# Delta rule on one core: two groups of heads half a level apart, products of one beside those of the other

## The chip, the cores and the metric

One core of a Trainium2 chip runs the whole program. The time is device microseconds of one execution; the median of three runs of the kernel before is 2759.25 us (2759.2 to 2761.63).

## The reference, cut to what matters

Two decoder layers run over 1024 tokens. The second one mixes tokens with the gated delta rule: eight heads, keys and values 128 wide. Each chunk solves a unit lower triangular system and passes a state on to the next chunk.

```python
a_mat = eye + where(strict, einsum('bhnid,bhnjd->bhnij', kb, k) * decay, 0)
sol = triangular_solve(a_mat, rhs, lower=True, unit_diagonal=True)   # -> u, w
attn = where(tri, einsum('bhnid,bhnjd->bhnij', q, k) * decay, 0)
def step(state, inp):
    v_new = u_n - w_n @ state
    o_n = qd_n @ state + attn_n @ v_new
    state = state * exp(gl_n) + kd_n^T @ v_new
```

The output o is divided by its root mean square, weighted, gated and projected.

## The kernel before, in words

`delta_rule` (from L4524) works in eight chunks of 128 tokens. All eight heads are on the chip together, in two groups of four (`q` = 0, the low group, heads 0 to 3; `q` = 1, the high group, heads 4 to 7). The inverse X of a chunk's triangular matrix is built by doubling: it begins with 2x2 blocks on the diagonal and joins pairs of blocks in six levels (`LEVELS`). For the first five levels a matrix of 128 rows is held as two blocks of 64, one on partitions 0 to 63 (`low`), one on 64 to 127 (`high`). A product of 64x64 operands uses one quarter of TensorE's array: its rows are the partitions that the operands lie on, its columns the partitions that the result is written to. A quarter is straight if both are the same half, and crosses if they differ. A quarter that crosses moves a block to the other half.

One level has two kinds of product. `products_b` (L4701, matmuls at L4716, at the last level L4713) multiplies B, the rest of the matrix, by X; `x_blk` holds X's blocks in the other half than `xt_blk` holds the transpose's, so all B products cross. `products_x` (L4719) multiplies the masked result by X's transpose, once straight (D, L4734) and once crossing (E, L4736), so it uses all four quarters; at the last level it is one crossing product per head (L4731). Each 64x64 product in float32 is two records in the trace, each with a weight load of its own.

Between them VectorE works, group by group: `mask_products` (L4981) takes B's result out of PSUM, times a mask, into `t_m`; `join` (L4989) subtracts E from `x_blk` (L4997) and D from `xt_blk` (L4998). At the last level `mask_products` is L4984 and `join` copies to `xt` (L4995).

The order on TensorE is written out by hand (from L4793). Per level both groups' B come first, then a block of other work, then both groups' X, then another such block. The blocks are 128-wide products for the same chunk, the next one or the one before: `k_state` (L4747) at levels 1 and 2, `outputs` of chunk n - 1 (L4760, L4761) at levels 2 and 3, `kk` of chunk n + 1 (L4671) at levels 3 and 4, `qk` (L4676) at levels 4 and 5. At the last level `first_x` (L4689, matmuls L4698) copies the next chunk's start into `first_ps` by products with the identity; `turn_out` (L4775, L4782) transposes the gated output of chunk n - 1; `new_values` (L4764, L4772) makes the chunk's new values; then come B of the next chunk's level 1 and `key_values` (L4785, L4790).

VectorE's order (from L5025) follows that of TensorE: both masks, other work, both joins. The other work is `next_state` (L5012) at level 1, `rests` (L5005) around levels 1 and 2, `sum_outputs` (L5014, a reduction of 128x1024 at L5018) behind level 3's joins, `decayed_keys` of chunk n + 1 (L4973) at level 4, `decayed_queries` (L4979) at levels 5 and 6.

ScalarE copies the outputs (`copy_y`, L4862), squares them (L4868), later scales the gated output (`finish_outputs`, L4892), moves B across the halves (`move_blocks`) and copies `first_ps` to `x_blk` (`copy_x`, L4917). GpSimd gates the output (`gate_outputs`, L5106), scales the next queries (L5076), computes the norm from the sum of squares (`output_norm`, L5112 and L5114), and only then makes the next chunk's first blocks (`start`, L5091 and L5093), which `first_x` waits for. All orders are fixed; engines wait for one another by semaphores alone, and an engine's queue stands still behind a wait.

Of the kernel before, what the change touches and what calls it, by code (L numbers as in the profile page):

```python
# [9 lines left out]
P = 128  # L10
# [4494 lines left out]
LEVELS = 6  # L4505
BLK = P // 2
# [17 lines left out]
def delta_rule(nc, feat, kv, gc_rows, gate_dram, norm_w, upper, ident, gates, gate_stored, kv_stored, a, following, chunk, late):  # L4524
# [14 lines left out]
    with ExitStack() as ctx:  # L4539
# [32 lines left out]

        t_ps, d_ps, e_ps, first_ps, last_ps = ([halves[:, b + q, e] for q in range(2)]
                                               for b, e in ((0, 0), (2, 0), (0, 1), (2, 1), (0, 1)))
        v_ps, c_ps, d4_ps = fours[2:4], fours[4:6], fours[6:8]
# [42 lines left out]
        def in_group(q):  # L4618
            return range(q * HG, (q + 1) * HG)

        @block.sync
# [43 lines left out]
        def _(pe):  # L4665
# [19 lines left out]
            def qk(m, q):  # L4685
                qk_opens(m, q)
                qk_heads(m, q, slice(0, HG)).then_inc(qk_done, 1)

            def first_x(m):  # L4689
                pe.wait_ge(start_done, m + 1)  # L4690
                if m > 0:
                    pe.wait_ge(x_joined, JV * m)
                    pe.wait_ge(xt_done, LV * m - 2)
                pe.sem_inc(tiles_seen, 1)
                for q in range(2):
                    for h in in_group(q):
                        for half, across in halves_across:
                            mm = pe.matmul(first_ps[q][across, h % HG], xt_blk[half, m % 2, h], ident[half, half], start=True, stop=True)  # L4698
                    mm.then_inc(x_done, 1)

            def products_b(n, l, q):  # L4701
                if l == 1:
                    pe.wait_ge(x_copied, 2 * n + q + 1)
                    pe.wait_ge(b_moved, 4 * n + 2 * q + 2)
# [5 lines left out]
                b = b_across[:, n % 2]  # L4710
                for h in in_group(q):
                    if l == LEVELS:
                        mm = pe.matmul(t_ps[q][high, h % HG], b[high, h, high], x_blk[high, h], start=True, stop=True)  # L4713
                    else:
                        for half, across in halves_across:
                            mm = pe.matmul(t_ps[q][half, h % HG], b[across, h, half], x_blk[across, h], start=True, stop=True)  # L4716
                mm.then_inc(t_done, 1)

            def products_x(n, l, q):  # L4719
                s = n % 2  # L4720
                pe.wait_ge(tm_done, LV * n + 2 * (l - 1) + q + 1)
                if l == 1:
                    pe.wait_ge(x_copied, 2 * n + 2)
                    if n > 0:
                        pe.wait_ge(v_copied, 2 * (n - 1) + q + 1)
                else:
                    pe.wait_ge(xt_done, LV * n + 2 * (l - 2) + q + 1)
                pe.sem_inc(tiles_seen, 1)
                for h in in_group(q):
                    if l == LEVELS:  # L4730
                        mm = pe.matmul(last_ps[q][low, h % HG], t_m[high, h], xt_blk[high, s, h], start=True, stop=True)  # L4731
                    else:
                        for half in (low, high):
                            pe.matmul(d_ps[q][half, h % HG], t_m[half, h], xt_blk[half, s, h], start=True, stop=True)  # L4734
                        for half, across in halves_across:
                            mm = pe.matmul(e_ps[q][across, h % HG], xt_blk[half, s, h], t_m[half, h], start=True, stop=True)  # L4736
                mm.then_inc(d_done, 1)

            def k_state(n, q):
# [34 lines left out]

            def turn_out(n):  # L4775
                pe.wait_ge(y_done, H * (n + 1))
# [4 lines left out]
                for h in range(H):  # L4781
                    mm = pe.transpose(c_both[:, h], gated[:, h], ident[:])  # L4782
                mm.then_inc(y_turned, 1)

# [13 lines left out]
            first_x(0)  # L4798
            for q in range(2):
                products_b(0, 1, q)  # L4800
            for n in range(TT):
                more = n + 1 < TT
                if n > 0:
                    for q in range(2):
                        key_values(n - 1, q)
                for l in range(1, LEVELS + 1):
                    if l > 1:
                        for q in range(2):
                            products_b(n, l, q)
                    if l == 2:  # L4810
                        k_state(n, 1)
                    if l == 3 and n > 0:
                        outputs(n - 1, 1)
                    if l == 4 and more:
                        kk(n + 1, 1)
                    if l == 5 and more:
                        qk_opens(n + 1, 1)
                        qk_heads(n + 1, 1, slice(0, HG // 2))
                    if l == LEVELS and more:
                        first_x(n + 1)  # L4820
                    for q in range(2):
                        products_x(n, l, q)
                    if l == 5 and more:
                        qk_heads(n + 1, 1, slice(HG // 2, HG)).then_inc(qk_done, 1)
                    if l == 1:
                        k_state(n, 0)
                    if l == 2 and n > 0:
                        outputs(n - 1, 0)
                    if l == 3 and more:
                        kk(n + 1, 0)  # L4830
                    if l == 4 and more:
                        qk(n + 1, 0)
                    if l == LEVELS and n > 0:
                        turn_out(n - 1)
                for q in range(2):
                    new_values(n, q)
                if more:
                    for q in range(2):
                        products_b(n + 1, 1, q)
            for q in range(2):  # L4840
# [3 lines left out]
        def _(act):  # L4844
# [72 lines left out]
            def copy_x(m):  # L4917
                if m > 0:
                    act.wait_ge(t_done, LV * m)
                for q in range(2):  # L4920
                    act.wait_ge(x_done, 2 * m + q + 1)
                    act.copy(group(x_blk, q), first_ps[q]).then_inc(x_copied, 1)

# [35 lines left out]
        def _(dve):  # L4959
# [21 lines left out]
            def mask_products(n, l, q):  # L4981
                dve.wait_ge(t_done, LV * n + 2 * (l - 1) + q + 1)
                if l == LEVELS:
                    dve.tensor_scalar(group(t_m[high], q), t_ps[q][high], -1.0, None, ALU.mult).then_inc(tm_done, 1)  # L4984
# [4 lines left out]
            def join(n, l, q):  # L4989
                s = n % 2  # L4990
                dve.wait_ge(d_done, LV * n + 2 * (l - 1) + q + 1)
                if l == LEVELS:
                    if n > 0:
                        dve.wait_ge(v_done, 2 * n)
                    dve.tensor_copy(group(xt[low, :, high], q), last_ps[q][low]).then_inc(xt_done, 1)  # L4995
                else:
                    dve.tensor_tensor(group(x_blk, q), group(x_blk, q), e_ps[q], ALU.subtract).then_inc(x_joined, 1)  # L4997
                    dve.tensor_tensor(group(xt_blk[:, s], q), group(xt_blk[:, s], q), d_ps[q], ALU.subtract).then_inc(xt_done, 1)  # L4998

# [25 lines left out]
            for n in range(TT):  # L5025
                more = n + 1 < TT
                for l in range(1, LEVELS + 1):
                    for q in range(2):
                        mask_products(n, l, q)
                    if l == 1 and n > 0:  # L5030
                        for q in range(2):
                            next_state(n - 1, q)
                    if l == 2:
# [3 lines left out]
                    if l == 5 and more:  # L5037
                        decayed_queries(n + 1, 0)
                    for q in range(2):
                        join(n, l, q)  # L5040
                    if l == LEVELS and more:
                        decayed_queries(n + 1, 1)
                    if l == 1:
                        rests(n, 0)
                    if l == 3 and n > 0:
                        sum_outputs(n - 1)
                    if l == 4 and more:
                        decayed_keys(n + 1, 1)
            following.split_lo(dve)

# [347 lines left out]
```

## Time and profile before

| | |
|---|---|
| median of three runs | 2759.25 us |
| the profiled execution, its own time | 2758.13 us |
| its span, first to last instruction | 2756.3 us |
| TensorE (PE) busy | 2673.5 us, 97% |
| VectorE (DVE) busy | 2116.3 us, 77% |
| ScalarE (ACT) busy | 1283.5 us, 47% |
| GpSimd (POOL) busy | 327.4 us, 12% |

The delta rule lies between about 1744 and 2002 us. In such rows stand the start in us from the span's first instruction, the duration, the engine, the line of the code, the operation with output and inputs, the shape and the number of instructions merged. PE is a matmul, PEld its weight load. A matmul's row ends when its result is written, so that successive rows overlap: the distance between starts tells what a product costs. What stands in square brackets at the end of a row is the engine's idle time before it and who ended it; "issue" means that the profile shows nothing that was waited for.

### The profile page before, as it was taken

Reading aid. Unit: us, or ns where it says so; the run is one execution under the profiler, and the core shown is the slowest. Engines: PE = TensorE matmul, PEld = TensorE weight load, DVE = VectorE, ACT = ScalarE, POOL = GpSimd, SP = SyncE. Lnnn points to the kernel's source line nnn. Section 1 sums busy time; section 2 is a strip of 40 time slices with the busy share of each in tenths; the row PEclk is TensorE's granted clock in tenths of the full one; section 3 lists DMA queues with packets and bytes.
Section 4 is the critical chain, followed back from the end, with each engine's and each line's share of the span. In section 5 each row is a group of like instructions: output and inputs, shape, how many; then the busy total and the mean of one; then the engine's idle time right before and its main releaser. Section 6 shows DMA issues by size and latency. Waiting matters only on the chain. (4 is left out here: it accounts for less than half of the span.)

```text
span 2756.3 us, 45813 instructions
## 1 busy us (share of the span) xinstructions
PE 2673.5 (97%) x17883; PEld 2240.5 (81%) x17883; DVE 2116.3 (77%) x3278; ACT 1283.5 (47%) x2296; POOL 327.4 (12%) x257
## 2 busy tenths in 40 slices
PE   9999989989999999999999999999999999999998
PEld 7888877778888888888878887888878888888886
DVE  6644456875799999897999975466658999998978
ACT  5333336842454444443456744566543544444332
POOL 0000045240000000000000001466411000000001
PEclk9999999999999999999999999999999999999999
DMA  5333253633412222475223423522042122225652
GB/s 186 122 107 107 92 195 114 170 123 110 147 54 92 85 81 80 159 265 187 92 93 121 158 76 123 196 95 96 16 176 101 69 92 77 84 92 188 226 185 88
DMA packets 162448, 339.15 MB, mean 123 GB/s; under 512 B 35584, under 2 KB 69568, under 8 KB 151616
## 3 DMA queue, kind: packets, MB, share of 16 engines
q1 hardware_dynamic: 144528, 324.69, 33.5%
q10 hardware_dynamic: 17712, 11.60, 1.4%
q8 instruction: 141, 2.31, 0.3%
q14 instruction: 67, 0.55, 0.1%
HBM read 252.17 MB, written 84.05 MB: 122 GB/s over the span
## 5 line engine op out<-in xcount | busy, mean ns | idle before, releaser
L2496 POOL TENSOR_TENSOR ffn_down_rstd<-ffn_down_rstd,ffn_down_power 128x1 f32<-128x1 f32 x15 | 15.0, 1000 | 1263.5 <-DVE ffn_down_rstd L2432 1263.5
L1053 DVE TENSOR_TENSOR even_in_w_lo<-even_in_raw_left,even_in_w_hi 128x512 fp32r<-128x512 f32 x80 | 49.9, 686 | 88.2 <-ACT even_in_w_hi L978 88.2
L936 PE MATMUL even_in_acc<-even_in_w_hi,even_x_hi 128*128 128x512 f32 x256 | 99.6, 389 | 0.0
L937 PE MATMUL even_in_acc<-even_in_w_lo,even_x_hi 128*128 128x512 f32 x256 | 99.6, 389 | 0.0
L938 PE MATMUL even_in_acc<-even_in_w_hi,even_x_lo 128*128 128x512 f32 x256 | 99.6, 389 | 0.0
L4040 DVE SCALAR_TENSOR_TENSOR even_mixed<-even_mixed,odd_qkv_taps 128x1023 f32<-128x1023 f32 (+2 forms) x72 | 92.1, 1281 | 4.9 <-ACT even_mixed L3873 3.2
L938 PE MATMUL even_in_acc<-even_in_w_hi,even_in_s_lo 128*128 128x512 f32 x192 | 74.7, 389 | 0.0
L936 PE MATMUL even_in_acc<-even_in_w_hi,even_in_s_hi 128*128 128x512 f32 x192 | 74.7, 389 | 0.0
L937 PE MATMUL even_in_acc<-even_in_w_lo,even_in_s_hi 128*128 128x512 f32 x192 | 74.7, 389 | 0.0
L3524 DVE CUSTOM_DVE_ANT_0 dil_probs<-dil_bank,dil_mask 128x128 f32<-128x128 f32 (+1 forms) x192 | 56.1, 347 | 22.3 <-PE dil_bank L3432 16.4
L3480 ACT ACTIVATE dil_probs<-dil_probs,dil_neg_peak 128x128 f32<-128x128 f32 (+1 forms) x192 | 70.7, 442 | 1.8 <-DVE dil_neg_peak L3529 1.8
L994 ACT COPY even_in_stage<-even_in_acc 128x512 f32<-128x512 f32 x48 | 28.2, 587 | 90.4 <-PE even_in_acc L938 83.2
L978 ACT CAST even_in_w_hi<-even_in_raw_left 128x512 fp32r<-128x512 f32 x80 | 43.7, 620 | 56.9 <-PE even_in_acc L938 56.9
L1225 ACT ACTIVATE odd_mixed<-odd_mixed,ffn_up_taps 128x1024 f32<-128x1024 f32 x44 | 54.5, 1245 | 32.9 <-DVE odd_mixed L1526 20.9
L1225 ACT ACTIVATE even_mixed<-even_mixed,ffn_up_taps 128x1024 f32<-128x1024 f32 x44 | 54.5, 1245 | 31.7 <-DVE even_mixed L1526 20.9
L4986 DVE TENSOR_TENSOR gdn_t_m<-gdn_bank,gdn_first_joins 128x256 f32<-128x256 f32 x80 | 33.2, 422 | 40.4 <-PE gdn_bank L4716 38.3
L2323 PE MATMUL ffn_down_acc<-four_hi,ffn_open_hi 128*128 128x512 f32 x160 | 62.3, 389 | 1.5 <-PEq L64 1.5
L2323 PE MATMUL ffn_down_acc<-two_hi,ffn_open_hi 128*128 128x512 f32 x160 | 62.4, 390 | 1.2 <-PEq L64 1.2
L1332 PE MATMUL ffn_up_tiles_acc<-ffn_up_tiles_t_hi,three_hi 128*128 128x512 f32 x160 | 62.4, 390 | 0.6 <-DVE three_lo L1490 0.6
L1332 PE MATMUL ffn_up_tiles_acc<-ffn_up_tiles_t_hi,one_hi 128*128 128x512 f32 x160 | 62.4, 390 | 0.6 <-DVE one_lo L1490 0.6
L2325 PE MATMUL ffn_down_acc<-two_hi,ffn_open_lo 128*128 128x512 f32 x160 | 62.3, 389 | 0.0
L2325 PE MATMUL ffn_down_acc<-four_hi,ffn_open_lo 128*128 128x512 f32 x160 | 62.3, 389 | 0.0
(877 smaller groups left out, 9095.6 us busy)
## 6 DMA issues: line engine op xcount, KB each, us to landing
ffn_w_raw<-in_ffn_up SPq DMA_DIRECT2D x42, 1024.0 KB, 4.8
even_mixed<-in_ffn_down SPq DMA_DIRECT2D x28, 512.0 KB, 4.4
odd_mixed<-in_ffn_down SPq DMA_DIRECT2D x28, 512.0 KB, 3.8
hp<-even_in_stage SPq DMA_DIRECT2D x13, 1024.0 KB, 4.2
hidden<-even_mixed SPq DMA_DIRECT2D x22, 512.0 KB, 2.6
ffn_w_raw<-in_od_w_qkv SPq DMA_DIRECT2D x11, 1024.0 KB, 5.7
hidden<-odd_mixed SPq DMA_DIRECT2D x22, 512.0 KB, 2.6
even_in_raw_left<-in_ev_w_in SPq DMA_DIRECT2D x10, 1024.0 KB, 5.3
```

What stands on the lines that cost most here:

```text
L936: pe.matmul(to, hi[:, tok], wh, start=(opens and k == 0), stop=False, skip_group_check=not opens)
L937: pe.matmul(to, hi[:, tok], wl, start=False, stop=False, skip_group_check=not opens)
L938: mm = pe.matmul(to, lo[:, tok], wh, start=False, stop=(k == KH - 1), skip_group_check=not opens)
L978: act.copy(w_hi[:, p % 2, k], source(i)[:, k]).then_inc(hi_ready, 1)
L1053: dve.tensor_tensor(w_lo[:, p % 2, k], source(i)[:, k], f32(w_hi[:, p % 2, k]), ALU.subtract).then_inc(lo_ready, 1)
L1225: act.activation(conv[:, g], c[:, g], ACT.Identity, bias=tap(j, g, FFN_CONV), scale=tap(j, g, FFN_CONV - 1)).then_inc(tap_done, 1)
L1332: mm = pe.matmul(result(m, i), ww[:, k], xx[:, k], start=(k == 0 and n == 0), stop=(k == KH - 1 and n == 2))
L2323: pe.matmul(bank(i, t), ah[:, tok], wh, start=begins, stop=False, skip_group_check=not opens)
L2325: return pe.matmul(bank(i, t), al[:, tok], wh, start=False, stop=ends, skip_group_check=not opens)
L3480: act.activation(p, p, ACT.Exp, bias=neg_peak[:, u % 2, h]).then_inc(exp_done, 1)
L3524: dve.tensor_tensor_reduce(probs[:, u % 2, h, k], s_ps[h][:, k], mask[:, kind(u), k], 1.0, -3e38, ALU.add, ALU.max, peak[:, u % 2, h]).the ...
L4040: dve.scalar_tensor_tensor(out=conv[:, g, back:SEQ], in0=c[:, g, 0:SEQ - back], scalar=tap(tile, GDN_CONV - 1 - back), in1=conv[:, g, back ...
```

## The change

Heads 0 and 1 become straight heads: their `x_blk` stays in its own half, so that their B products run on straight quarters and their E products too, with results in PSUM places of their own (`t_first`, `t_straight`, `t_last`, `e_straight`). `copy_x` takes heads 0 and 1 in one copy and the other six in another. On VectorE the low group's masks and x joins become two instructions each.

On TensorE the two groups are half a level apart. `low_x_high_b(n, l)` issues the low group's X and the high group's B of level l, alternating; `high_x_low_b(n, l)` issues the high group's X of level l and then the low group's B of level l + 1. Between these two stand the blocks of other work, in the order as before. At the last level the low group's B and X come earlier than the high group's; `turn_out` is cut in two, one half behind each of the two B or X groups; `key_values` of the high heads waits for the first mask, since `t_first` lies in its bank. VectorE's order becomes group by group as well, and `sum_outputs` stands behind level 4's low join.

```diff
+        first_ps = [bank[:, 2 + i].rearrange("p (h t) -> p h t", t=BLK) for i in range(2)]
+        e_straight, t_straight, t_first, t_last = halves[:, 2, 1], halves[:, 3, 1], halves[:, 7, 0], halves[:, 1, 0]
...
+            def b_head(n, l, h):
+                for half, across in halves_across:
+                    if straight(h):
+                        mm = pe.matmul(t_to(l, h)[half], b_mat[half, n % 2, h, half], x_blk[half, h], start=True, stop=True)
+                    else:
+                        mm = pe.matmul(t_to(l, h)[half], b_across[across, n % 2, h, half], x_blk[across, h], start=True, stop=True)
+                return mm
...
+            def e_head(n, h):
+                for half, across in halves_across:
+                    to = e_straight[half, h] if straight(h) else e_ps[h // HG][across, h % HG]
+                    mm = pe.matmul(to, xt_blk[half, n % 2, h], t_m[half, h], start=True, stop=True)
+                return mm
...
+            def high_x_low_b(n, l):
+                high_x(n, l)
+                if l == 1 and n > 0:
+                    pe.wait_ge(v_copied, 2 * n)
+                products_b_open(n, l + 1, 0)
+                b_head(n, l + 1, 0)
+                b_head(n, l + 1, 2)
+                b_head(n, l + 1, 1)
+                b_head(n, l + 1, 3).then_inc(t_done, 1)
+
+            def low_x_high_b(n, l):
+                products_x_open(n, l, 0)
+                pe.sem_inc(tiles_seen, 1)
+                d_head(n, 0)
+                e_head(n, 2)
+                d_head(n, 1)
+                e_head(n, 3)
+                products_b_open(n, l, 1)
+                d_head(n, 2)
+                b_head(n, l, 4)
+                d_head(n, 3)
+                b_head(n, l, 5)
+                e_head(n, 0)
+                b_head(n, l, 6)
+                e_head(n, 1).then_inc(d_done, 1)
+                b_head(n, l, 7).then_inc(t_done, 1)
...
                 if n > 0:
-                    for q in range(2):
-                        key_values(n - 1, q)
...
+                    key_values(n - 1, 0)
+                    pe.wait_ge(tm_done, LV * n + 1)
+                    key_values(n - 1, 1)
+                low_x(n, 1)
+                k_state(n, 0)
+                high_x_low_b(n, 1)
+                k_state(n, 1)
+                low_x_high_b(n, 2)
+                if n > 0:
+                    outputs(n - 1, 0)
+                high_x_low_b(n, 2)
...
+                low_x_high_b(n, 5)
+                if more:
+                    qk_heads(n + 1, 1, slice(HG // 2, HG)).then_inc(qk_done, 1)
+                high_x(n, 5)
+                last_b(n, 0)
+                if n > 0:
+                    turn_out(n - 1, 0)
+                last_x(n, 0)
+                last_b(n, 1)
+                if more:
+                    first_x(n + 1)
+                last_x(n, 1)
+                if n > 0:
+                    turn_out(n - 1, 1)
...
+                join_x(n, 1, 0)
+                join_xt(n, 1, 0)
+                rests(n, 0)
+                for l in range(2, LEVELS):
+                    mask_products(n, l, 0)
+                    join_x(n, l - 1, 1)
+                    join_xt(n, l - 1, 1)
                     if l == 2:
                         rests(n, 1)
                     if l == 4 and more:
                         decayed_keys(n + 1, 0)
                     if l == 5 and more:
                         decayed_queries(n + 1, 0)
...
+                    dve.wait_ge(d_done, LV * n + 2 * (l - 1) + 1)
+                    mask_products(n, l, 1)
+                    join_x(n, l, 0)
+                    join_xt(n, l, 0)
+                    if l == 4 and n > 0:
                         sum_outputs(n - 1)
                     if l == 4 and more:
                         decayed_keys(n + 1, 1)
+                mask_products(n, LEVELS, 0)
+                join_x(n, LEVELS - 1, 1)
+                join_xt(n, LEVELS - 1, 1)
+                if more:
+                    decayed_queries(n + 1, 1)
+                join_last(n, 0)
+                mask_products(n, LEVELS, 1)
+                join_last(n, 1)
```

`low_x` is `low_x_high_b` without B (level 1), `high_x` the high group's X as before, `last_b` and `last_x` the last level's products of one group, `first_b` level 1's B of both.

## Rows read from the trace of the kernel before

**Rows 1.** The page's first line.

```profile
span 2756.3 us, 45813 instructions
```

**Rows 2.** Timeline of TensorE in a middle chunk, levels 3 and 4.

```profile
1862.12 0.39 PE L4761 MATMUL gdn_bank<-gdn_v_new,gdn_attn 128*128 128x128 f32 x2
1862.43 0.27 PE L4734 MATMUL gdn_bank<-gdn_xt_blk,gdn_t_m 64*64 64x64 f32 x2
...
1862.49 0.14 PEld L4734 LDWEIGHTS gdn_bank<-gdn_xt_blk,gdn_t_m 64*64 64x64 f32 x2
...
1863.37 0.23 PE L4736 MATMUL gdn_bank<-gdn_t_m,gdn_xt_blk 64*64 64x64 f32 x2
1863.53 1.16 PE L4671 MATMUL gdn_bank<-gdn_first_x_t 128*128 128x128 f32 x8
1864.62 1.15 PE L4716 MATMUL gdn_bank<-gdn_x_blk,gdn_b_across 64*64 64x64 f32 x32
1865.69 1.16 PE L4671 MATMUL gdn_bank<-gdn_first_x_t 128*128 128x128 f32 x8
```

**Rows 3.** The same timeline: the same chunk's first_x, and a quiet chunk's ends.

```profile
1874.12 0.27 PE L4698 MATMUL gdn_bank<-top_ident,gdn_xt_blk 64*64 64x64 f32 x2
...
1938.94 1.95 PE L4772 MATMUL gdn_bank<-gdn_u,gdn_xt 128*128 128x128 f32 x16
...
1966.08 1.15 PE L4698 MATMUL gdn_bank<-top_ident,gdn_xt_blk 64*64 64x64 f32 x32 [0.37 <-POOL gdn_xt_blk L5093]
...
1969.02 1.95 PE L4772 MATMUL gdn_bank<-gdn_u,gdn_xt 128*128 128x128 f32 x16
```

**Rows 4.** Timelines of ACT, POOL and DVE beside rows 2, the same chunk.

```profile
1862.54 0.58 ACT L4862 COPY gdn_y<-gdn_bank 128x512 f32<-128x512 f32 x1 [2.47 <-PE gdn_bank L4761]
...
1863.26 2.37 POOL L5106 TENSOR_TENSOR gdn_gated<-gdn_y,gdn_gate 128x1024 f32<-128x1024 f32 x1 [2.02 <-issue]
1865.59 2.37 POOL L5076 TENSOR_TENSOR gdn_q_et<-gdn_first_x_t,gdn_exp_row 128x1024 f32<-128x1024 f32 x1
1867.91 0.20 POOL L5112 TENSOR_TENSOR gdn_o_norm<-gdn_o_sumsq,top_q_eps 128x8 f32<-128x8 f32 x1
1868.19 1.65 POOL L5114 TENSOR_TENSOR gdn_o_norm<-gdn_o_norm,gdn_power 128x8 f32<-128x8 f32 x1
1870.01 2.62 POOL L5091 TENSOR_TENSOR gdn_xt_blk<-gdn_b_mat,gdn_first_c 64x512 f32<-64x512 f32 x2 [0.17 <-POOL gdn_o_norm L5114]
1872.71 1.27 POOL L5093 TENSOR_TENSOR gdn_xt_blk<-gdn_xt_blk,gdn_unit_c 128x512 f32<-128x512 f32 x1
...
1863.20 0.42 DVE L4997 TENSOR_TENSOR gdn_x_blk<-gdn_x_blk,gdn_bank 128x256 f32<-128x256 f32 x1 [2.20 <-PE gdn_bank L4736]
1863.54 0.41 DVE L4998 TENSOR_TENSOR gdn_xt_blk<-gdn_xt_blk,gdn_bank 128x256 f32<-128x256 f32 x1
...
1864.53 1.21 DVE L5018 TENSOR_REDUCE gdn_o_sumsq<-gdn_squares 128x8 f32<-128x1024 f32 x1
```

**Rows 5.** Timelines of TensorE and DVE: first and last chunk's v products, a mask and its X.

```profile
1783.91 2.02 PE L4772 MATMUL gdn_bank<-gdn_u,gdn_xt 128*128 128x128 f32 x16 [0.24 <-DVE gdn_xt L4995]
...
1996.87 1.95 PE L4772 MATMUL gdn_bank<-gdn_u,gdn_xt 128*128 128x128 f32 x16
...
1990.63 0.42 DVE L4986 TENSOR_TENSOR gdn_t_m<-gdn_bank,gdn_first_joins 128x256 f32<-128x256 f32 x1
...
1991.19 0.27 PE L4734 MATMUL gdn_bank<-gdn_xt_blk,gdn_t_m 64*64 64x64 f32 x2
```

**Rows 6.** Timeline of TensorE: an idle time that the profile ascribes to nothing.

```profile
1872.43 0.21 PE L4734 MATMUL gdn_bank<-gdn_xt_blk,gdn_t_m 64*64 64x64 f32 x1 [0.61 <-issue]
```

**Rows 7.** Groups of instructions kept apart by shape, VectorE, another stage's masking from PSUM.

```profile
L3524 DVE CUSTOM_DVE_ANT_0 dil_probs<-dil_bank,dil_mask 128x256 f32<-128x256 f32 x88 | 32.0, 419 | 10.8 <-PE dil_bank L3432 9.4 <-DVE dil_gathered L3569 1.3 <-PE dil_bank L3423 0.2
L3524 DVE CUSTOM_DVE_ANT_0 dil_probs<-dil_bank,dil_mask 128x128 f32<-128x128 f32 x104 | 24.0, 285 | 11.5 <-PE dil_bank L3432 7.1 <-DMA dil_mask<-in_dil_masks 3.4 <-DVE dil_part L3569 1.0
```

More of the change, by code:

```diff
@@ new lines, in d_head @@
+            def d_head(n, h):
+                for half in (low, high):
+                    pe.matmul(d_ps[h // HG][half, h % HG], t_m[half, h], xt_blk[half, n % 2, h], start=True, stop=True)
+            def e_head(n, h):
+                for half, across in halves_across:
+                    to = e_straight[half, h] if straight(h) else e_ps[h // HG][across, h % HG]
+                    mm = pe.matmul(to, xt_blk[half, n % 2, h], t_m[half, h], start=True, stop=True)
+                return mm
@@ L4728, in products_x, with last_x @@
+            def last_x(n, q):
+                products_x_open(n, LEVELS, q)
                 pe.sem_inc(tiles_seen, 1)
                 for h in in_group(q):
[L4730 to L4736, printed above, removed]
@@ L4737, in products_x @@
-                mm.then_inc(d_done, 1)
+                    mm = pe.matmul(last_ps[q][low, h % HG], t_m[high, h], xt_blk[high, n % 2, h], start=True, stop=True)
+                mm.then_inc(d_done, 1)
+            def high_x_low_b(n, l):
[7 more added lines that the diff above has]
+                b_head(n, l + 1, 3).then_inc(t_done, 1)
@@ L4798, in _ @@
             first_x(0)
-            for q in range(2):
-                products_b(0, 1, q)
+            first_b(0)
             for n in range(TT):
@@ L4919, in copy_x @@
                     act.wait_ge(t_done, LV * m)
-                for q in range(2):
-                    act.wait_ge(x_done, 2 * m + q + 1)
-                    act.copy(group(x_blk, q), first_ps[q]).then_inc(x_copied, 1)
+                for i, some in enumerate((slice(0, 2), slice(2, H))):
+                    act.wait_ge(x_done, 2 * m + i + 1)
+                    act.copy(x_blk[:, some], first_ps[i][:, some]).then_inc(x_copied, 1)
             def copy_out(n):
@@ L4983, in mask_products @@
                 if l == LEVELS:
-                    dve.tensor_scalar(group(t_m[high], q), t_ps[q][high], -1.0, None, ALU.mult).then_inc(tm_done, 1)
+                    if q == 0:
+                        dve.tensor_scalar(t_m[high, 0:2], t_last[high, 0:2], -1.0, None, ALU.mult)
+                    some = slice(2, HG) if q == 0 else slice(0, HG)
+                    dve.tensor_scalar(group(t_m[high], q)[:, some], t_ps[q][high, some], -1.0, None, ALU.mult).then_inc(tm_done, 1)
+                elif q == 0:
+                    mask = joins[:, l - 1].unsqueeze(1).broadcast_to([P, 2, BLK])
+                    dve.tensor_tensor(t_m[:, 0:2], (t_first if l == 1 else t_straight)[:, 0:2], mask, ALU.mult)
+                    dve.tensor_tensor(t_m[:, 2:HG], t_ps[0][:, 2:HG], mask, ALU.mult).then_inc(tm_done, 1)
                 else:
```

158 lines of the change are left out of this document (87 added, 71 removed).

## The prediction

> **What bounds the kernel now.** I read the page first: the profiled execution spans 2756.3 us [rows 1], the time beside it is 2758.13 us, and the sum below is made against that 2758.13; it lies 1.1 us under the median of the runs, 2759.25. The change touches one stage, the delta rule, eight chunks of 128 tokens. Second, TensorE's timeline in one chunk [rows 2]. The reader is to see that there is no idle time: X products run from 1862.43, the last pair starts at 1863.37, the 128-wide block of the next chunk's keys follows at 1863.53, B at 1864.62, the next block at 1865.69. The 64 X records (two per product) take 0.94 us, 0.0585 us for every four; the 32 B records take the same time, since B uses only the two quarters of the array that cross from one half of the partitions to the other. I call 0.0585 us a step: X of both groups is 16 steps, B of both groups 16. A level is X, a block of other work, B and another such block: 1.10, 1.09, 1.07 and again 1.09, so 4.35 us [rows 2].
>
> Third, the end of a chunk [rows 3]. In the quiet chunk between the first v product at 1938.94 and the next at 1969.02 (30.08 us) TensorE does wait once: first_x at 1966.08, 0.37 us, for POOL's xt_blk. So I read the other engines along what leads there [rows 4]: the last output product of the chunk starts at 1862.12 [rows 2], ACT copies y at 1862.54, POOL gates it at 1863.26, scales the next queries at 1865.59, takes the norm at 1867.91 and its power at 1868.19, builds the next chunk's start from 1870.01 and 1872.71, ends it at 1873.98, and first_x comes 0.14 later, at 1874.12. That is 12.00 us from the last output to first_x, and first_x to the next chunk's outputs is TensorE alone. The stage is bound by a loop through both engines.
>
> To price the change I went through the orders of TensorE, VectorE, ScalarE and GpSimd as the code has them, each instruction with its duration from these rows: VectorE starts 0.27 to 0.29 after the last product it needs starts (the low group's X ends with the eighth step, at 1862.91; the join starts at 1863.20), 128x256 instructions leave 0.33 apart, a product starts 0.14 after the VectorE instruction it needs has ended (1991.05 to 1991.19) [rows 4, 5]. For the kernel before this gives 29.99 us per full chunk: 29.10 of TensorE's own work and 0.89 of waiting for POOL. The quiet chunk shows 30.08. The last chunk, which has no next chunk to fill its gaps, comes to 26.25. From the first chunk's v product to the last one's that is 206.31 us; the trace has 212.96 [rows 5]. The 6.65 us left over are idle times that no row explains, like the 0.61 before 1872.43 that ends by "issue" [rows 6].
>
> **The change, part by part.** *B beside X.* In levels 2 to 5 the low group's B runs in four quarters (4 steps instead of 8), and the high group's B runs on the quarters that the low group's X leaves free: 12 steps for both where 8 and 8 stood. A level is 24 steps, not 32: 8 x 0.0585 x 4 levels = 1.87 us per chunk. Level 1 gains nothing: its B saves 4 steps, its low X, with nothing beside it, loses 4. Products, weight loads and DMAs stay as many; no moved step issues a DMA, and SP's loads, which wait for keys, queries and gate of the chunk before, are released within 2 us of their old place and used a chunk later: nothing for them.
>
> *The transposes of the output in two halves.* One more change from 64-wide to 128-wide work and back: 0.15 in (1863.38 to 1863.53 [rows 2]), 0.21 back, an estimated 0.06 for the slower first step of each of the two blocks (the sixteenth step of X starts 0.94 after the first, where 15 steps are 0.88 [rows 2]), less the two steps that stood there, 0.15: 0.32 us. The low group's last B, half overlapping, saves a step. TensorE's own work falls by 1.87 - 0.32 + 0.06 = 1.61, from 29.10 to 27.49.
>
> *VectorE's halves.* Eleven instructions per chunk become two, since heads 0 and 1 lie in another bank. No row in this stage has that shape from PSUM; another stage's masking from PSUM takes 285 ns at 128x128 and 419 at 128x256 [rows 7], and 419 is also what the joins take here [rows 4]. I take 0.285 and starts 0.20 apart, the nearest row; a gain is excluded, a half costing a whole (0.42) is the upper end, which adds 4.5 us over the stage.
>
> *VectorE's new order, the part that decides.* The sum of squares (1.21 us, at 1864.53 [rows 4]) moves from behind level 3's joins to behind level 4's low join, and the group-wise order puts that join behind the mask of level 4's high group. Count from the last output product. TensorE: low X of level 3 from 0.20, keys, half-level from 2.13, keys, low X with high B of level 4 from 4.06 to 4.75. VectorE: mask at 5.02, the two half joins 5.35 and 5.55, the other join 5.75, the sum from 6.08 to 7.29. POOL would be free for the norm at 5.79 (1867.91 less 1862.12); before, the sum was done at 3.62 (1865.74). Now the norm starts at 7.34, and 6.21 later (1867.91 to 1874.12) first_x: 13.55 instead of 12.00. TensorE is there at 12.84 and waits 0.72. Behind the sum VectorE also has the key decay (0.62) and then level 5's low mask, done at 8.33; TensorE is free at 7.48 and starts low X of level 5 at 8.47: 0.99 of waiting, with qk, X and B of levels 5 and 6 queued behind. Smaller waits (0.05, 0.09, 0.20) follow at level 5's high B, its high X and level 6's low X. ScalarE's scaling of the gated output is 1.5 later with the norm; the transposes still find it done, by 0.4 us.
>
> The other half of the loop, first_x to the last output, loses 28 of 112 steps (8 of X that now stand ahead of first_x, 4 of B in level 1, 8 in each of the two rounds of X and B that follow: 1.64) and four transposes that now stand ahead of first_x (4 x 0.093): 17.99 becomes 15.97. So a chunk takes 15.97 + 13.56 = 29.53 against 29.99: 0.46 won out of 1.61. The added wait on the low group's mask between the two key-value blocks costs nothing: the mask is over 0.6 us before it.
>
> *The last chunk.* From level 3 no block covers VectorE's round trip. Before, one group's products cover the other's masks; now each half-level ends, then 0.27 + 0.42 + 0.14 pass, 0.77 more than a step, twice a level. Going through it the same way gives 27.34 against 26.25: 1.09 lost.
>
> *Sum.* 6 x 0.46 - 1.09 = 1.7 us less. The unexplained 6.65 I leave as it is: as many instructions in about the same time. 2758.13 - 1.7 = 2756.4, on the scale of the median 2757.6 us. A measurement of this kernel can tell about 0.2% (5.5 us) from no change, so this is no change.
>
> **A rule against it.** In the X block, weight loads for both kinds of product on the same rows run while products on those rows are under way (loads at 1862.49 between products that start at 1862.43 and last 0.27) and four records still pass per step [rows 2]. The Trainium skill, "TensorE: Matmul & The Clock Gate", Part 3, says that a weight load overlaps products in flight only where the row group differs; by it the other group's B would queue behind D and E on the same rows. The trace speaks against it for X, where D and E share rows.
>
> **The rivals.** *Unpaired B, slower.* If the high group's B doesn't run beside the low group's X, that half-level is 20 steps, not 12, and the loop comes to 30.94 a chunk: 10.3 us more than before, 2769.5 us. It decides (5.5 us slower) once some six in ten of these steps are unpaired. For it: two groups' operands were never mixed in one block. Against it: D, E and both halves mix at full rate now [rows 2]. Chance 0.10; it is also the case that the change doesn't do what it says.
>
> *The sum is not in the way, faster.* If VectorE reaches the sum earlier, or POOL is held by something else than the rows show, the two waits of 0.99 and 0.72 go and a chunk takes some 28.4: 9.3 us less, 2750 us. For it: this count rests on waits that no row of before shows. Against it: for the quiet chunk of before it is right to 0.1 us. Chance 0.16.
>
> *The unexplained idle time moves.* The blocks are denser now. If it falls from 6.65 to near nothing, 2751 (0.09); if it doubles, 2764.3, and with halves on VectorE at the price of a whole 4.5 more, 2768.8 (0.07).
>
> **How the numbers follow.** The forecast, within 5.5 us of the median, has 0.58. Faster 0.16 + 0.09 = 0.25, slower 0.10 + 0.07 = 0.17. The range takes in the two faster cases and the doubled idle time with a third of the dearer halves, 2749 to 2766, and leaves out the unpaired B.
>
> **What would show it.** Right: low X and high B as one run of 48 records in about 0.7 us; sum of squares ending about 7.3 us after the last output; first_x waiting for POOL in nearly every chunk; X of level 5 waiting for its mask about 1 us; chunks 29.5 apart when quiet; the last chunk longer than before. Wrong: that run at 1.0 us or more (unpaired), or POOL's norm starting under 6 us after the last output and chunks near 28.

## The result and the profile after

The changed kernel took 2766.36 us (median of 20 runs, 2753.68 to 2774.93), the kernel before 2760.72 in its 20 runs beside them: a ratio of 1.0022 with a 95% interval of 1.0013 to 1.0030. It is slower by 5.6 us where 1.7 us less and "no change" was forecast; the median lies 0.4 us above the range.

The first lines of the page after; [rows 1] is what answers to the span.

```profile
span 2763.5 us, 45876 instructions
...
PE 2671.2 (97%) x17883; PEld 2234.1 (81%) x17883; DVE 2119.3 (77%) x3366; ACT 1284.0 (46%) x2296; POOL 328.9 (12%) x257
```

TensorE is busy 2.3 us less and the span is 7.2 us longer. The timelines of TensorE, VectorE, GpSimd and ScalarE in one quiet chunk after, 1848.29 to 1878.30, answer to [rows 2 to 4]:

```profile
1848.29 0.35 PE L4857 MATMUL gdn_bank<-gdn_u,gdn_xt 128*128 128x128 f32 x1
...
1862.32 0.39 PE L4846 MATMUL gdn_bank<-gdn_v_new,gdn_attn 128*128 128x128 f32 x2
1862.64 0.27 PE L4731 MATMUL gdn_bank<-gdn_xt_blk,gdn_t_m 64*64 64x64 f32 x2
...
1863.34 0.23 PE L4726 MATMUL gdn_bank<-gdn_x_blk,gdn_b_across 64*64 64x64 f32 x2
1863.50 1.16 PE L4676 MATMUL gdn_bank<-gdn_first_x_t 128*128 128x128 f32 x8
...
1871.04 0.27 PE L4731 MATMUL gdn_bank<-gdn_xt_blk,gdn_t_m 64*64 64x64 f32 x2 [0.99 <-DVE gdn_t_m L5084]
...
1876.20 0.95 PE L4703 MATMUL gdn_bank<-top_ident,gdn_xt_blk 64*64 64x64 f32 x32 [0.71 <-POOL gdn_xt_blk L5212]
...
1878.30 0.35 PE L4857 MATMUL gdn_bank<-gdn_u,gdn_xt 128*128 128x128 f32 x1
...
1865.58 0.29 DVE L5083 TENSOR_TENSOR gdn_t_m<-gdn_bank,gdn_first_joins 128x128 f32<-128x128 f32 x1 [0.70 <-PE gdn_bank L4726]
...
1868.69 1.21 DVE L5125 TENSOR_REDUCE gdn_o_sumsq<-gdn_squares 128x8 f32<-128x1024 f32 x1
...
1869.98 0.20 POOL L5231 TENSOR_TENSOR gdn_o_norm<-gdn_o_sumsq,top_q_eps 128x8 f32<-128x8 f32 x1 [1.81 <-DVE gdn_o_sumsq L5125]
...
1877.89 0.65 ACT L5015 COPY gdn_x_blk<-gdn_bank 128x128 f32<-128x128 f32 x2
```

The mechanism is the predicted one. Low X and high B, 48 records, run from 1862.64 to the last pair at 1863.34, and the next block starts at 1863.50. The last output product is the two records of the row at 1862.32; the forecast's times count from the second, at 1862.43. The sum ends 7.47 us after it (forecast 7.29), POOL's norm starts after 7.55 (7.34) with 1.81 us of waiting for it, level 5's X waits 0.99 (0.99) for its mask, first_x 0.71 (0.72) for POOL. A half on VectorE takes 0.28 to 0.29 us (0.285). But the chunk takes 30.0 us, not 29.53.

Put side by side, the distances between the first v products of successive chunks, read from the timelines, the last one being the last chunk:

| kernel | us | sum |
|---|---|---|
| before | 30.59 31.37 31.18 31.26 30.62 30.08 27.85 | 212.96 |
| after | 34.04 32.67 30.02 33.02 31.36 30.02 29.62 | 220.74 |

The 7.8 us between the sums are all of the 7.2 by which the span grew. They are not in the quiet chunks, 30.08 and 30.02, but in the disturbed ones. Two things disturb them. The first is in the view of waits, TensorE alone, 1784 to 1990 us (us in total, times, longest); of after:

```profile
PE gdn_bank L4731 <- DVE gdn_t_m L5084: 6.2, 6, 1.3
PE gdn_bank L4857 <- issue: 3.8, 2, 2.5
PE gdn_bank L4703 <- POOL gdn_xt_blk L5212: 3.6, 5, 0.7
PE gdn_bank L4876 <- issue: 2.4, 2, 1.7
...
PE gdn_bank L4726 <- issue: 0.5, 1, 0.5
```

and of before:

```profile
PE gdn_bank L4734 <- issue: 2.5, 3, 1.2
PE gdn_bank L4716 <- issue: 1.8, 2, 1.5
PE gdn_bank L4736 <- issue: 1.5, 2, 1.3
PE gdn_bank L4734 <- DVE gdn_t_m L4986: 1.4, 1, 1.4
PE gdn_bank L4698 <- POOL gdn_xt_blk L5093: 1.0, 2, 0.6
...
PE gdn_bank L4747 <- issue: 0.3, 1, 0.3
```

Idle time by "issue", the kind of [rows 6], is 6.1 us of 9.0 before and 6.7 of 17.2 after, so it stayed; VectorE's and POOL's waits came on top. The second is the granted clock. The rows by windows (length, busy time of each engine, PEclk, DMA share, GB/s), of after:

```profile
1904.00:1911.00 7.00, 6.96 (x105) 6.24 (x105) 3.85 (x12) 5.39 (x13) 5.72 (x5) 0.52 0.80 255
...
1996.00:2007.00 11.00, 10.39 (x96) 9.63 (x97) 3.00 (x9) 5.09 (x13) 2.05 (x1) 0.53 0.01 1
```

and of before:

```profile
1904.00:1911.00 7.00, 7.00 (x119) 6.69 (x120) 3.39 (x10) 4.24 (x10) 2.90 (x3) 1.00 0.78 245
...
1996.00:2007.00 11.00, 8.62 (x66) 8.30 (x66) 4.13 (x6) 7.07 (x11) 0.00 (x0) 0.91 0.08 23
```

After, TensorE is granted 1.2 GHz for nearly all of these two stretches, just behind idle times (1.0 and 0.5 us in the 2.5 us up to 1903.41; 0.7 to 1.3 us five times in the last chunk before 1996); before, it keeps 2.4 GHz through the first and up to 2005.0 in the second. A third such stretch, 1788.2 to 1791.6, follows a single idle time of 1.74 us by "issue". From level 5's X to the next v product a chunk needs 6.96 us at 1.2 GHz (1904.36 to 1911.32) and 5.60 at 2.4 (1872.70 to 1878.30).

What is behind "issue"? The longest one cuts a run of eight equal v products (sixteen records), in a place where no new wait stands. TensorE's timeline after:

```profile
1815.62 1.69 PE L4857 MATMUL gdn_bank<-gdn_u,gdn_xt 128*128 128x128 f32 x13
1819.80 0.49 PE L4857 MATMUL gdn_bank<-gdn_u,gdn_xt 128*128 128x128 f32 x3 [2.50 <-issue]
```

and the DMA view of after, first from 1811 to 1817 us, then from 1817 to 1818.5 (queue and kind: packets, MB, share of 16 engines; a packet counts whole where it starts, so a share can pass 100%):

```profile
q1 hardware_dynamic: 2176, 1.97, 102.2%
...
q1 hardware_dynamic: 30, 0.13, 21.2%
q8 instruction: 1, 0.02, 4.5%
```

While x_t and x of a coming chunk, 2.1 MB, fill the sixteen engines, no packet of the instruction queue passes; the 16 KB of instructions come with the tail of the burst, ending at 1818.52, and the product follows 1.3 us later. It is the same everywhere: all fourteen idle times by "issue" between the first and the last v product, nine before and five after, end 1.3 to 1.6 us behind such a 16 KB packet, and each lies, counted in the trace, a multiple of 256 TensorE instructions (to within one) from the others of its kernel. That made the theory for the experiments: the late sum costs the waits, the chunk loads make TensorE's code late, and waits and late code together lower the clock. The trace of after already speaks against so simple a rule for the clock: from 1807 to 1820 idle times of 1.27, 0.75 and 2.50 us follow one another and it stays at 2.4 GHz. Rival: the idle time by "issue" is TensorE's own, and the sum alone decides.

### The profile page after: what moved, and what is told of

Read it like the earlier page. It is cut to its first block and busy times, and to the rows that moved or that the text cites. A ratio compares the mean times of both kernels' runs of the same rounds, so it can differ in the third digit from the quotient of the medians.

```text
span 2763.5 us, 45876 instructions
## 1 busy us (share of the span) xinstructions
PE 2671.2 (97%) x17883; PEld 2234.1 (81%) x17883; DVE 2119.3 (77%) x3366; ACT 1284.0 (46%) x2296; POOL 328.9 (12%) x257
## 5 line engine op out<-in xcount | busy, mean ns | idle before, releaser
L994 ACT COPY even_in_stage<-even_in_acc 128x512 f32<-128x512 f32 x48 | 28.3, 589 | 90.3 <-PE even_in_acc L938 83.7
L4731 PE MATMUL gdn_bank<-gdn_xt_blk,gdn_t_m 64*64 64x64 f32 x1280 | 56.3, 228 | 13.1 <-DVE gdn_t_m L5084 9.2
L4731 PEld LDWEIGHTS gdn_bank<-gdn_xt_blk,gdn_t_m 64*64 64x64 f32 x1280 | 45.6, 137 | 23.6 <-issue 17.0
L4736 PE MATMUL gdn_bank<-gdn_t_m,gdn_xt_blk 64*64 64x64 f32 x1280 | 62.7, 228 | 0.0
```

What stands on the lines that cost most here:

```text
L4731: pe.matmul(d_ps[h // HG][half, h % HG], t_m[half, h], xt_blk[half, n % 2, h], start=True, stop=True)
L4736: mm = pe.matmul(to, xt_blk[half, n % 2, h], t_m[half, h], start=True, stop=True)
```

## The experiments

Each run's kernel before ran on the same chip beside it.

**The sum of squares a level earlier**, in the changed kernel.

```diff
-                    if l == 4 and n > 0:
+                    if l == 3 and n > 0:
                         sum_outputs(n - 1)
```

> The changed kernel with the sum of squares back behind level 3 (behind the low group's join of level 3). Theory 1 (the late sum holds GpSimd and the masks, and the idle time on TensorE that follows costs its clock): the 1.26 us gap before level 5's low X and the 0.92 us gap before first_x close to under 0.4 us, quiet chunks are 28.1 us apart instead of 30.0, fewer stretches at half clock; 10 to 14 us faster than the changed kernel, some 6 to 10 faster than the kernel before (ratio to before 0.996 to 0.998). Theory 2 (denser TensorE work makes late starts without a cause, 'issue', more frequent): the gaps close, but the idle time ended by 'issue' grows by as much, and the time stays within 4 us of the changed kernel's.

Measured: 2760.37 us, ratio to before 1.0000 (0.9987 to 1.0013). Quiet chunks fell to 28.33 to 28.40 as expected, but four of seven took 31.1 to 31.6: the waits view has 7.7 us of "issue" here, and the last chunk ran at 1.2 GHz for 17 us. Moving the sum back is worth 6 us where 10 to 14 were expected; the idle time by "issue" is still there.

**The unfilled places filled**: two products with the identity matrix in the seven places of the first and the last chunk where no block of other work stands, their results overwritten.

```diff
+            def fill(n):
+                if n > 0:
+                    pe.wait_ge(y_copied, 2 * (n - 1) + 1)
+                for i in range(2):
+                    pe.matmul(d4_ps[0][:, i], ident[:], ident[:], start=True, stop=True)
...
+                else:
+                    fill(n)
```

> The changed kernel with two 128-wide products of the identity (unused result) in each of the seven places of the first and last chunk where no block of other work stands. Theory 1: these take the place of idle time that the walk already has (0.77 us each), so nothing is added; the clock stays at 2.4 GHz in the last chunk, whose distance falls from 29.6 to about 27.5 us, and the last outputs run in 3.4 us instead of 4.3; 3 to 5 us faster than the changed kernel, about even with the kernel before. Theory 2: no change, or slower by the products' own 4 us.

Measured: 2763.56 us, 1.0010 (0.9998 to 1.0021). The last chunk took 27.83 us, 1.8 less, and the stage ran 10 us at 1.2 GHz instead of 27. The clock is part of it; the middle chunks still took up to 33.6.

**Both together.**

> Both edits together. Theory 1: the gains add, 13 to 17 us faster than the changed kernel and 9 to 12 us faster than the kernel before (ratio 0.9955 to 0.997). Theory 2: within 4 us of the changed kernel.

Measured: 2760.39 us, 1.0001 (0.9990 to 1.0011). The two gains did not add up: quiet chunks 28.34, but others of 30.3 to 34.3. My expectation had left out that the code could be later still: its waits view has 10.9 us of "issue".

**The kernel before with the late sum** (behind level 4's joins).

```diff
-                if l == 3 and n > 0:
+                if l == 4 and n > 0:
                     sum_outputs(n - 1)
```

> The kernel before with one edit alone: the sum of squares behind level 4's joins instead of level 3's. Theory 1: chunks 32.05 us apart instead of 29.99 when quiet, with a wait of first_x for GpSimd of about 3 us in each; 13 us slower, and more if the clock falls in these waits, ratio 1.004 to 1.008. Theory 2: VectorE has idle time in this kernel, so the place of the sum costs nothing, ratio 1.000.

Measured: 2782.94 us, 1.0082 (1.0065 to 1.0099), so 22.6 us slower. In a middle chunk first_x now waits 2.01 us for POOL (about 3 was expected), and 37.5 us of the stage ran at 1.2 GHz. The place of the sum is a heavy price by itself, more than the waits alone.

**Small chunk loads**, in three kernels: the test of late code. From the third chunk on only 16 of 128 rows of x_t, x and the gate are fetched (the gate's lines are not shown); the rest is left out, so the stage computes with older data. gc_row, 0.5 MB, is loaded whole as ever.

```diff
-                sp.dma_start(x_t[:, s], feat[:, :, m * P:(m + 1) * P].rearrange("h d t -> d h t")).then_inc(x_t_in[s], 16)
+                rows = slice(0, P if m < 2 else 16)
+                sp.dma_start(x_t[rows, s], feat[:, rows, m * P:(m + 1) * P].rearrange("h d t -> d h t")).then_inc(x_t_in[s], 16)
...
-                sp.dma_start(x[:, s].rearrange("p h d -> p (h d)"), kv[m]).then_inc(x_in[s], 16)
+                sp.dma_start(x[rows, s].rearrange("p h d -> p (h d)"), kv[m][rows]).then_inc(x_in[s], 16)
```

> The kernel before, in which the loads of x_t, x and the gate for the chunks from the third on fetch 16 of 128 partitions (the other partitions keep the data of two chunks earlier, so the numbers computed are other ones; the instructions are the same). Theory 'late code': TensorE's idle time without a releaser, some 8 us between the first and the last new_values in the trace of before, is its next 16 KB of instructions held up behind 2.1 MB and 1 MB of chunk loads on the DMA engines. Without the load bursts the gaps of 0.8 to 1.8 us at the instruction blocks vanish, the chunks take 29.5 us each but the last, 206.3 in place of 212.96 us in all, and the time is 2753 to 2755 us. Rival 'the idle time is TensorE's own (its queue or its array)': the gaps stay, 2760 us.

> The changed kernel with the same small loads (the same part of the computation on older data). Theory 'late code and the clock': the late sum's waits (1.0 us before X5 low, 0.9 before first_x) stay in every chunk, the code gaps go; chunks of 30.0 us in place of 30.0 to 34.0, and the half clock follows only the unfilled places of the first and the last chunk: 2756 to 2760 us, still slower than the kernel before with small loads by some 2 to 5 us. If the waits alone set the half clock in the middle chunks, it stays and the time is 2763 us or more. Rival 'TensorE's own': 2766.

> The changed kernel with the sum of squares a level earlier, the seven unfilled places filled and the small loads (the same part of the computation on older data). Theory 'late code': all chunks but the first at 28.3 to 28.4 us and the last at 27.5, the sum from the first to the last new_values 197 to 199 us against 212.96, so 2744 to 2748 us: what the stagger saves is there as soon as the code comes in time. Rival 'what is won in a chunk is given back somewhere else': 2756 to 2760.

Measured: before 2752.54 us, 0.9975 (0.9964 to 0.9986); after 2756.04, 0.9985 (0.9976 to 0.9994); early and filled 2746.05, 0.9946 (0.9933 to 0.9959). The times are the theory's (the first 0.5 us under its range); the chunks in the trace of before with small loads are not, 30.06 us and more where 29.5 was expected. The waits view of after with small loads, the same stretch, whole:

```profile
PE gdn_bank L4734 <- DVE gdn_t_m L5087: 8.3, 8, 1.3
PE gdn_bank L4706 <- POOL gdn_xt_blk L5215: 4.3, 6, 0.7
PE gdn_bank L4734 <- DVE gdn_t_m L5089: 2.2, 3, 0.7
PE gdn_bank L4797 <- DVE gdn_t_m L5083: 0.8, 1, 0.8
PE gdn_bank L4870 <- ACT gdn_gated L4988: 0.2, 1, 0.2
```

No row by "issue" is left, and the waits of the late sum all are. Its chunks: 30.43, then 30.01 or 30.02 five times, and 28.14; those of before with small loads 30.06 to 30.17 but for one of 32.06, and 27.57 (some 3 us of "issue" remain there; the longest, 1.8 us, stands behind the burst of gc_row). With the early sum and the filled places they take 28.33 to 29.76, 1.5 us of "issue" among them, and 27.82. The rows by windows of after with small loads:

```profile
1777.00:1960.00 183.00, 170.43 (x4008) 153.92 (x4008) 116.62 (x325) 126.75 (x332) 117.91 (x73) 1.00 0.08 23
```

Six chunks with idle times of 1.0 and 0.7 us each, and the clock stays at 2.4 GHz. In this execution the waits alone don't lower it, nor in that of the changed kernel with paced loads below, from 1770 to 1981 us. But this one is the shortest of the eleven, 2749.03 us at a mean clock of 0.995; their median is 2756.04 at 0.993, an estimated 11 us more at 1.2 GHz (0.002 of 2756 us, at half the clock), and where in the program those lie no trace shows.

**The whole loads in pieces**: x_t and x in four parts, gate and gc_row in two, 256 KB each, and SP waits for the next B products of TensorE before each part (shown for x_t).

```diff
+            def after_products(n, l, q):
+                if LV * n + 2 * (l - 1) + q + 1 > 0:
+                    sp.wait_ge(t_done, LV * n + 2 * (l - 1) + q + 1)
...
+                for i in range(4):
+                    after_products(m - 3 + i // 2, 6 if i < 2 else 1, i % 2)
+                    cut = slice(i * H // 2, (i + 1) * H // 2)
+                    sp.dma_start(x_t[:, s, cut], feat[cut, :, m * P:(m + 1) * P].rearrange("h d t -> d h t")
+                                 ).then_inc(x_t_in[s], 16)
```

With the early sum and the filled places:

> The changed kernel with the sum of squares a level earlier, the seven places filled, and the whole chunk loads in twelve pieces of 256 KB (x_t in four, x in four, gate and gc_row in two each), each piece waiting for the next half level's B products of TensorE, so that no burst is longer than about 0.9 us (two pieces at a chunk's start 1.8). Theory 'late code': an instruction block is delayed by at most a piece, which its lead of some 2 to 2.5 us covers: 2745 to 2751 us, faster than both kernels. Rival 'loads' volume, not their bursts, delays the code': 2756 to 2760 us, with as many gaps, only spread.

Measured: 2745.47 us, 0.9951 (0.9939 to 0.9963): faster than both kernels, with the whole computation. The DMA view from 1840 to 1870 us shows as many bytes as ever (3.36 MB; after has 3.05 from 1848 to 1878), and six instruction packets that pass among them; the waits view, whole, has no "issue" (it lists idle times from 0.15 us up):

```profile
q1 hardware_dynamic: 3692, 3.36, 36.9%
q8 instruction: 6, 0.10, 1.3%
...
PE gdn_bank L4839 <- DVE gdn_t_m L5145: 1.8, 5, 0.6
PE gdn_bank L4776 <- DVE gdn_t_m L5149: 0.7, 1, 0.7
```

Chunks: 28.51 to 28.80, last 27.81. So the bursts delay the code, not the volume.

The same pieces in the kernel before, in the changed kernel as it is, and with the early sum alone:

> The kernel before with the whole chunk loads in twelve paced pieces of 256 KB. If the pacing takes away the late code and nothing else, this is the kernel before with small loads (2752.5 us): chunks of 30.1 us, 2751 to 2755 us. Then what the stagger adds of its own is the distance of the next run to this one. If the paced pieces themselves win or lose something (SP's waits, more transfers), it is off that number.

> The changed kernel as it is, with the paced loads. Theory 'the late sum and ScalarE's chain take back what the pairs save': chunks of 30.0 us with idle of 1.05 us at X5 low and 0.9 at first_x in each, last chunk 28 to 28.3 (its waits of 0.9 to 1.5 us without a filler): 2754 to 2758 us, 0 to 5 us slower than the kernel before with paced loads. The prediction's own sum says 1.7 us faster than that one.

> The changed kernel with the sum of squares a level earlier and the paced loads, the seven places of the first and the last chunk left unfilled. Inner chunks of 28.5 us as in the run with the places filled. Theory 'the short waits of the last chunk alone bring the half clock': the last chunk takes 29 to 31 us and the time is 2747 to 2751. If they do so only on top of late code, the last chunk takes 28 and the time is 2744 to 2747.

Measured: before 2759.63 us, 0.9993 (0.9982 to 1.0003); after 2756.75, 0.9982 (0.9973 to 0.9991); early 2749.77, 0.9959 (0.9941 to 0.9976). After's time came out as expected, before's did not: its two groups' B products come together, so each pair of pieces went out 0.4 to 0.5 us apart, as a burst of 0.5 MB, and idle times by "issue" of 2.1 and 0.7 us remain. The distance between these two therefore says nothing of the stagger; the one with small loads says more. With the early sum alone the last chunk took 27.67 us at full clock, and after as it is, with the same idle places there, 30.55 (28 to 28.3 was expected). The early sum's result is divided: by its median it falls to the theory that the short waits alone bring the lower clock, by the last chunk of its trace, an execution of 2746.16 us, to the other. The rows by windows of the last chunk's second part, after with pieces and then early with pieces:

```profile
1979.00:1997.00 18.00, 14.98 (x206) 14.02 (x207) 6.92 (x21) 6.97 (x15) 4.19 (x3) 0.62 0.01 2
...
1976.00:1992.00 16.00, 11.67 (x232) 10.54 (x224) 8.32 (x21) 8.73 (x17) 3.10 (x2) 1.00 0.01 2
```

**The pairs undone**, on top of the paced kernel with the early sum and the filled places.

```diff
                 e_head(n, 3)
-                products_b_open(n, l, 1)
                 d_head(n, 2)
-                b_head(n, l, 4)
                 d_head(n, 3)
...
+                products_b_open(n, l, 1)
+                for h in in_group(1):
+                    mm = b_head(n, l, h)
```

> As the paced run with the early sum and the filled places, but at each of the four inner half levels the low group's X products all come first and the high group's B products behind them, not one head of B beside one of X. The prediction took 1.87 us per chunk as what the pairs save: chunks of 30.0 to 30.4 us in place of 28.5, 2757 to 2761 us. If a 64 x 64 product goes as fast alone as beside one on other quarters: 28.5 and 2745 us.

Measured: 2751.36 us, 0.9963 (0.9952 to 0.9975), 0.0012 more than with pairs, and 29.39 us in a quiet chunk against 28.33 to 28.58. TensorE's timeline without pairs, one such block and the product that follows:

```profile
1906.87 0.27 PE L4776 MATMUL gdn_bank<-gdn_xt_blk,gdn_t_m 64*64 64x64 f32 x2
...
1907.57 0.51 PE L4771 MATMUL gdn_bank<-gdn_x_blk,gdn_b_across 64*64 64x64 f32 x11
1908.01 0.38 PE L4889 MATMUL gdn_bank<-gdn_state,gdn_q_et 128*128 128x128 f32 x1
```

From first product to what follows it is 1.14 us, with pairs 0.86 (1880.44 to 1881.30 in the run with the early sum and pieces): 0.28, four times a chunk, is 1.12, and the chunks show 0.8 to 1.1. The 1.87 that I expected here was a misreading of my own sum: half of it belongs to the low group's B in four quarters, which this edit leaves alone.

## Why the prediction was wrong

**B beside X: right.** 48 records in 0.71 us, as forecast; TensorE's own work per chunk comes to 27.5 us (27.49): 30.0 less what its blocks stand farther apart than where nothing is waited for, 1.06 at level 5's X, 0.87 at first_x, 0.27 at the v products and 0.16 at each of level 5's high X and level 6's low X. The rule weighed there (the Trainium skill, "TensorE: Matmul & The Clock Gate", Part 3), by which B would queue behind products on the same rows, is not borne out by this block. Unpaired, a half level takes 17 steps (1.14 less the 0.15 into the next block is 0.99, by 0.0585), not the 20 of the rival, so D and E share the quarters better alone than I counted. That rival's 10.3 us also doesn't follow from its own terms: 6 x 0.95 for the full chunks and 1.09 + 1.87 for the last are 8.7.

**The late sum: right.** It was the part that decides, and its times came out within 0.2 us. Undoing it gives 28.33 to 28.40 us in a quiet chunk (forecast "near 28", 28.4 in the rival).

**The chunk at 29.53: 0.48 short.** POOL's norm is 0.21 late. ScalarE scales the gated output, moves B's blocks, places xt and only then copies x (1877.89), so that v products start 0.38 us behind the transposes, not 0.11: 0.27. The prediction followed ScalarE to the transposes, not past them to new_values. And a slip in the sum: 12.00 counts from the first record of the last output product (1862.12), 7.34 and with it 13.55 from the second (1862.23), so 0.11 was lost, and 29.64 would have been its own result. The three make 0.59, 0.11 more than is missing.

**The last chunk at 27.34: 28.14 at full clock but for its last 0.7 us** (small loads), 29.62 in the changed kernel. Before, it was 27.57 and not 26.25. (And 6 x 29.99 + 26.25 are 206.19, not 206.31.)

With these the undisturbed chunks come to 30.43 + 5 x 30.02 + 28.14 = 208.7 us after (the first chunk waits 1.3 us for level 5's mask) and 6 x 30.06 + 27.57 = 207.9 before: 0.7 more instead of 1.7 less, still no change.

**The step that failed: "The unexplained 6.65 I leave as it is."** Above the undisturbed sums the traces have 5.0 us before and 12.1 after. That is the rival "the unexplained idle time moves", doubled: 2764.3 us, to which I gave 0.07. The idle time is TensorE's code behind the chunk loads, which the small and the paced loads take away (10 us less in the changed kernel). Late code itself did not grow: from the first to the last v product it is 6.8 us before and 6.7 after. What grew is its price, in two ways. The first is the clock: TensorE is granted 1.2 GHz for 27 us of the stage instead of 7. The three stretches between the first and the last v product cost, against the same work at 2.4 GHz, 1.4 us (1904: 6.96 less 5.60), 1.5 (the last chunk: 29.62 less 28.14) and an estimated 1.7 at most (half of 3.4 us at 1788): some 4.5 of the 7.1 us. The second is the waits. Before, first_x waits 0.4 to 0.6 us for POOL in a quiet chunk and not at all in the four chunks with most late code, which stands in place of that wait: of the 6.8 us 5.0 reach the sum. After, first_x still waits in five of six chunks, so the two add up. Late code and clock make 11.2 of the 12.1 us; the other 0.9 I can't assign to a row.

Not settled: what makes the clock fall. One stop of 1.74 us was followed by it (1788), idle times of 1.27, 0.75 and 2.50 us in a row were not (1807 to 1820); it fell in the last chunk of one paced kernel and not of the other, which idle in the same places, and the one that kept it had no wait over 0.31 us in the chunks before. The account above is also of one execution of each kernel: the mean clock is 0.990 in the trace of after and 0.992 in the median of its 20 runs, 0.996 in the trace of before and 0.994 to 0.995 in the medians of its runs beside the experiments, so the clock's part of the 5.6 us is likely smaller than between these two. The same goes for the small loads: by the traces the undisturbed chunks are nearly equal, by the medians the changed kernel is 3.5 us slower (ratios 0.9985 and 0.9975, with overlapping intervals), and its trace is its shortest execution.

## What to carry to other kernels

Idle time that the profile gives to "issue", in the middle of a block of equal products, can be late code: look whether an instruction packet lands just before it ends, and what filled the DMA engines until then. A large load that nobody waits for is not free; here, with the sum at its old level and the unfilled places filled, cutting it into pieces paced by the engine's own progress made a kernel that gained nothing into one that gains 14 us. And an idle time is priced with what stands beside it: in the kernel before late code took the place of a wait, in the changed one it came on top, and in its trace three idle stretches were followed by TensorE's lower clock for the work behind them.

## What was unexpected of the hardware

An instruction packet of 16 KB, 1.1 us on its queue, came only with the tail of a 2.1 MB burst, and TensorE stood idle up to 2.9 us (with the early sum) though nothing waited for that load. With 256 KB pieces that go out one at a time no such idle time over 0.6 us is left. The clock held 2.4 GHz through six chunks with 1.0 and 0.7 us of idle in each (window row 1777 to 1960); in the trace of after it fell behind 1.0 and 0.5 us close together (1904), behind 1.74 us (1788), and in the last chunk with five idle times of 0.7 to 1.3 us. The order of the same 24 products alone changes their time from 0.86 to 1.14 us.
